# Stick-breaking attention in one core's three-block model: constant products split in halves, value projection moved among the heads

## What is computed

```
z = einsum(q_block, k_upto_end) * 64 ** -0.5
mask = s_pos < t_pos
log_1m = where(mask, log_sigmoid(-z), 0)
tail = cumsum(log_1m, reverse) - log_1m          # sum over s < j < t
w = where(mask, exp(log_sigmoid(z) + tail), 0)
y[t] = sum_s w[t, s] * v[s]
```

## Time and profile before

| | us |
|---|---|
| median of 3 runs (lowest to highest) | 3806.75 (3800.33 to 3807.62) |
| the profiled execution | 3799.45 |
| its span | 3798.1 |
| PE busy in the span | 3574.1 |
| DVE, ACT, POOL busy | 2016.2, 1440.3, 350.3 |
| the stage from the end of q and k to the first gate | 1664.5 to 1791.9 |

### The profile page before, as it was taken

How to read it: one execution, slowest core, us unless ns; L and a number is a source line. 1 busy time by engine, 2 the same in 40 slices (tenths; PEclk the granted TensorE clock), 3 DMA queues, 4 the chain that set the end, 5 groups by cost and what they waited for, 6 DMA issues and landing times. The chain is left out here.

```text
span 3798.1 us, 44034 instructions
## 1 busy us (share of the span) xinstructions
PE 3574.1 (94%) x16956; PEld 2892.0 (76%) x16956; DVE 2016.2 (53%) x3283; ACT 1440.3 (38%) x2555; POOL 350.3 (9%) x346
## 2 busy tenths in 40 slices
PE   8999989999998999989999989998899998989999
PEld 7877777877776887767887778877776777867877
DVE  4546465678436324731334466666465475563256
ACT  2224343355523223436223353354343232343244
POOL 1000000013001100012010100000000123111101
PEclk9999999999999999999999999999999999999999
DMA  6445311221223324420322232254201220132255
GB/s 235 181 172 178 118 45 52 72 67 34 95 89 107 132 94 135 164 66 12 106 80 72 95 100 95 95 173 142 86 23 49 72 78 12 39 112 88 93 180 166
DMA packets 106126, 380.15 MB, mean 100 GB/s; under 512 B 11760, under 2 KB 14592, under 8 KB 105792
## 3 DMA queue, kind: packets, MB, share of 16 engines
q1 hardware_dynamic: 100944, 364.86, 29.2%
q0 software_dynamic: 2896, 10.38, 0.9%
q10 hardware_dynamic: 2080, 2.10, 0.2%
HBM read 375.19 MB, written 2.10 MB: 99 GB/s over the span
## 5 line engine op out<-in xcount | busy, mean ns | idle before, releaser
L396 DVE TENSOR_TENSOR w_low<-ring,w_high 128x1024 fp32r<-128x1024 f32 x637 | 810.8, 1274 | 1011.0 <-ACT w_high L384 1003.4
L420 PE MATMUL bank<-x_low,w_high 128*128 128x512 f32 (+1 forms) x2560 | 999.9, 394 | 58.3 <-DVE w_low L396 15.9
L384 ACT ACTIVATE w_high<-ring 128x1024 fp32r<-128x1024 f32 x637 | 670.6, 1053 | 899.2 <-PE bank L420 377.6
L420 PE MATMUL bank<-x_high,w_low 128*128 128x512 f32 (+1 forms) x2560 | 988.4, 390 | 0.0
L420 PE MATMUL bank<-x_high,w_high 128*128 128x512 f32 (+1 forms) x2560 | 635.2, 386 | 0.0
L420 PEld LDWEIGHTS bank<-x_low,w_high 128*128 128x128 f32 x2560 | 494.7, 193 | 162.5 <-issue 23.9
L420 PEld LDWEIGHTS bank<-x_high,w_low 128*128 128x128 f32 x2560 | 495.6, 194 | 97.2 <-issue 1.4
L420 PEld LDWEIGHTS bank<-x_high,w_high 128*128 128x128 f32 x2560 | 466.4, 192 | 99.2 <-issue 1.9
L482 PE MATMUL bank<-w_low,x_high 128*128 128x512 f32 (+3 forms) x416 | 156.8, 377 | 1.3 <-ACT z_z L1693 1.3
L484 PE MATMUL bank<-w_high,x_high 128*128 128x512 f32 (+3 forms) x416 | 155.7, 374 | 0.0
L483 PE MATMUL bank<-w_high,x_low 128*128 128x512 f32 (+3 forms) x416 | 155.7, 374 | 0.0
(11 more groups left out here) (626 smaller groups left out, 5669.1 us busy)
## 6 DMA issues: line engine op xcount, KB each, us to landing
ring<-in_W SPq DMA_DIRECT2D x688, 512.0 KB, 3.5
f_hid<-in_xT ACTq DMA_DIRECT2D x2, 1024.0 KB, 11.6
X<-in_x POOLq DMA_DIRECT2D x1, 2048.0 KB, 10.7
out<-X SPq DMA_DIRECT2D x4, 512.0 KB, 4.2
const<-in_consts POOLq DMA_DIRECT2D x1, 1389.0 KB, 7.0
f_norm<-in_ln_g POOLq DMA_DIRECT2D x2, 512.0 KB, 8.6
f_norm<-in_ln_b POOLq DMA_DIRECT2D x2, 512.0 KB, 10.9
ring<-in_W SPq DMA_DIRECT2D x2, 432.0 KB, 3.1
```

The costliest lines, as they stand in the source:

```text
L384: ac.activation(b.UH[i % NU][:, 0:src.shape[1]], src, ACT.Copy).then_inc(*b.split.act.up("high", i))
L396: dv.tensor_tensor(b.UL[i % NU][:, 0:n], src, b.UH[i % NU][:, 0:n].bitcast(F32), SUB).then_inc(*b.split.dve.up("low", i))
L420: i = pe.matmul(out, w[:, k, c], v, start=n == 0 and q == 0, stop=last and q == 3 * K - 1)
```

## The change

1. The products of line 2085 are taken of two fp32r halves of `B1`: `BH` (high) and `BL` (low), against fp32r copies `nge`, `nones` of the constants, which are exact in that type. Identity and `neg` get fp32r copies as well. VectorE makes the halves of head r-1 in round r, `BH` over the place of `A1` and `BL` over that of `B1`; its semaphore `halves` takes the place of GpSimd's `sp` for TensorE. `A1` has three buffers where it had two.
2. The value projection `v2` moves from ahead of the rounds to round 1, after the scores of head 1. Its conversions (ScalarE, VectorE) and copies into `VP` move with it; TensorE waits for `v` only ahead of head 0's output, but waits for `k` ahead of the first scores.
3. In a round TensorE takes the scores first, then the log weights, then the output. ScalarE takes the absolute value, exponential and logarithm of head r first, then the exponential of the log weights of head r-2. VectorE splits outputs one round later, at the end of its round.

```diff
 def tensor_stick(b, s):
     pe.wait_ge(*s.gq.act.at("q", 3))
-    pe.wait_ge(*s.gq.dve.at("v", 3))
-    pe.wait_ge(*b.arrived("const2"))
+    pe.wait_ge(*s.gq.dve.at("k", 7))
     for r in range(8 + 3):
+        h = r            # scores, as before
...
+        if r == 1:
+            tensor_rows(b, s.gq, "v2", b.x, lambda t: b.bank(("v2", t), s.gq.dve.at("v", t)))
+            pe.wait_ge(*g.dve.at("signs"))
+        h = r - 2
...
+                pe.matmul(bank.ap[:, 0:wd], s.KP[:, j, l, c0:c0 + 128], s.QT[:, j, c0:512], start=True, stop=False)
+                pe.matmul(bank.ap[:, 0:128], s.eye, s.neg, start=False, stop=False)
+                if i == 0:
+                    pe.wait_ge(*g.dve.at("halves", h))
+                for jj in range(i, 4):
+                    sl = slice(OFF2[jj], OFF2[jj] + WID2[jj])
+                    sign, out = s.nge if jj == i else s.nones, bank.ap[:, 128 * (jj - i):wd]
+                    pe.matmul(out, sign, s.BL[h % 3][:, sl], start=False, stop=False)
+                    x = pe.matmul(out, sign, s.BH[h % 3][:, sl], start=False, stop=jj == 3)
...
+            if h == 0:
+                pe.wait_ge(*s.gq.dve.at("v", 3))
 def scalar_stick(b, s):
+            a1 = s.A1[h % 3]
+            if h >= 3:
+                ac.wait_ge(*g.pe.at("logw", h - 3, 3))
...
+        if r < 2:
+            for k in V2_AHEAD[r]:
+                scalar_ahead(b, ("v2", "w", k))
 def vector_stick(b, s):
+    for x, name in ((s.nge, "nge"), (s.nones, "nones"), (s.neg, "neg")):
+        dv.tensor_copy(x, b.const(name)).then_inc(*f.up())
+    dv.tensor_copy(s.eye, b.ident).then_inc(*f.up("signs"))
+    def halves(h):
+        b1, high, low = s.B1[h % 3], s.BH[h % 3], s.BL[h % 3]
+        dv.wait_ge(*g.pool.at("sp", h))
+        dv.tensor_copy(high, b1).then_inc(*f.up("high", h))
+        dv.wait_ge(*f.at("high", h))
+        dv.tensor_tensor(low, b1, high.bitcast(F32), SUB).then_inc(*f.up("halves", h))
...
+        if r < 2:
+            for k in V2_AHEAD[r][:1]:
+                vector_ahead(b, ("v2", "w", k))
+        if 1 <= r < 9:
+            halves(r - 1)
+        if r == 1:
+            for k in V2_AHEAD[r][1:]:
+                vector_ahead(b, ("v2", "w", k))
+            vector_v2(b, s)
```

More of the change, by code:

```diff
@@ L1911, in __init__ @@
         gates = Area(b, a.at)
-        self.A1 = [a.take("a2_a", 1280) for _ in range(2)]
-        self.B1 = [a.take("a2_b", 1280) for _ in range(3)]
+        over = Area(b, a.at)
+        self.A1, self.B1 = ([a.take(f"a2_{n}", 1280) for _ in range(3)] for n in "ab")
+        self.BH, self.BL = ([over.take(f"a2_b{n}", 1280, dtype=F32R) for _ in range(3)] for n in "hl")
         self.W1 = [a.take("a2_w", 1280) for _ in range(2)]
         self.sinc = a.take("a2_sinc", 128)
+        self.nge, self.nones, self.neg, self.eye = (a.take(f"a2_{n}", 128, dtype=F32R) for n in ("nge", "nones", "neg", "eye"))
         self.YAH, self.YAL = a.take("a2_yh", 4, 512, dtype=F32R), a.take("a2_yl", 4, 512, dtype=F32R)
@@ L2006, in tensor_qkv2 @@
         tensor_tile(b, g, ("q2", m), [("q2", m)], 0, b.x, bank.ap)
-    tensor_rows(b, g, "v2", b.x, lambda t: b.bank(("v2", t), g.dve.at("v", t)))
 def scalar_qkv2(b, s):
@@ L2016, in scalar_qkv2 @@
             ac.activation(s.QT[:, m, :], b.bk["q2", m], ACT.Copy, scale=0.125).then_inc(*g.act.up("q", m))
-    scalar_rows_ahead(b, "v2")
 def vector_qkv2(b, s):
@@ L2028, in vector_qkv2, with vector_v2 @@
             dv.tensor_copy(s.KP[64:128, m - 4, 1, :], b.bk["q2", m][64:128, :]).then_inc(*g.dve.up("k", m))
-    vector_rows_ahead(b, "v2")
+def vector_v2(b, s):
+    dv, g = b.nc.vector, s.gq
     dv.wait_ge(*g.pool.at("v_zero"))
@@ L2049 @@
 WID2 = [512, 384, 256, 128]
+V2_AHEAD = ((0,), (2, 4, 6))
 def tensor_stick(b, s):
@@ L2054, in tensor_stick @@
     pe.wait_ge(*s.gq.act.at("q", 3))
-    pe.wait_ge(*s.gq.dve.at("v", 3))
-    pe.wait_ge(*b.arrived("const2"))
+    pe.wait_ge(*s.gq.dve.at("k", 7))
     for r in range(8 + 3):
+        h = r
+        if h < 8:
+            j, l = h // 2, h % 2
+            for i in range(4):
+                bank = b.bank(("ss", h, i), g.dve.at("pos", h, i))
+                for e in bank.emptied:
+                    pe.wait_ge(*e)
+                c0 = 128 * i
+                pe.matmul(bank.ap[:, 0:WID2[i]], s.KP[:, j, l, c0:c0 + 128], s.QT[:, j, c0:512], start=True,
+                          stop=True).then_inc(*g.pe.up("scores", h, i))
+        if r == 1:
+            tensor_rows(b, s.gq, "v2", b.x, lambda t: b.bank(("v2", t), s.gq.dve.at("v", t)))
+            pe.wait_ge(*g.dve.at("signs"))
+        h = r - 2
+        if 0 <= h < 8:
+            j, l = h // 2, h % 2
+            for i in range(4):
+                bank = b.bank(("sw", h, i), g.act.at("w", h, i))
+                for e in bank.emptied:
+                    pe.wait_ge(*e)
+                c0, wd = 128 * i, WID2[i]
+                pe.matmul(bank.ap[:, 0:wd], s.KP[:, j, l, c0:c0 + 128], s.QT[:, j, c0:512], start=True, stop=False)
[7 more added lines that the diff above has]
+                    x = pe.matmul(out, sign, s.BH[h % 3][:, sl], start=False, stop=jj == 3)
+                x.then_inc(*g.pe.up("logw", h, i))
         h = r - 3
@@ L2071, in tensor_stick @@
                 b.drop(("so", j))
[L2072 to L2097, removed]
 def scalar_stick(b, s):
@@ L2102, in scalar_stick @@
     for r in range(8 + 2):
+        h = r
+        if h < 8:
+            a1 = s.A1[h % 3]
+            if h >= 3:
+                ac.wait_ge(*g.pe.at("logw", h - 3, 3))
+            for i in range(4):
+                ac.wait_ge(*g.pe.at("scores", h, i))
+                ac.activation(a1[:, OFF2[i]:OFF2[i] + WID2[i]], b.bk["ss", h, i][:, 0:WID2[i]],
+                              ACT.Abs).then_inc(*f.up("abs", h, i))
+            ac.wait_ge(*f.now())
+            ac.activation(a1, a1, ACT.Exp, scale=-1.0).then_inc(*f.up())
+            ac.wait_ge(*f.now())
+            ac.activation(a1, a1, ACT.Ln, bias=1.0).then_inc(*f.up("log", h))
+        if r < 2:
+            for k in V2_AHEAD[r]:
+                scalar_ahead(b, ("v2", "w", k))
         h = r - 2
@@ L2110, in scalar_stick @@
                               ACT.Exp).then_inc(*f.up("w", h, i))
[L2111 to L2123, removed]
 def vector_stick(b, s):
@@ L2129, in vector_stick @@
     dv.tensor_scalar(s.sinc, b.const("neg"), 0.0, None, ALU.is_equal).then_inc(*f.up("sinc"))
[L2130 to L2137, removed]
+    for x, name in ((s.nge, "nge"), (s.nones, "nones"), (s.neg, "neg")):
[7 more added lines that the diff above has]
+        dv.tensor_tensor(low, b1, high.bitcast(F32), SUB).then_inc(*f.up("halves", h))
+    for r in range(8 + 4):
         h = r
@@ L2146, in vector_stick @@
                                  MAX).then_inc(*f.up("pos", h, i))
+        if r < 2:
[7 more added lines that the diff above has]
+            vector_v2(b, s)
+        h = r - 4
+        if 0 <= h < 8 and h % 2:
+            j = h // 2
+            dv.wait_ge(*g.pe.at("out", h))
+            dv.tensor_copy(s.YAH[:, j, :], b.bk["so", j]).then_inc(*f.up("yhigh", j))
+            dv.wait_ge(*f.at("yhigh", j))
+            dv.tensor_tensor(s.YAL[:, j, :], b.bk["so", j], s.YAH[:, j, :].bitcast(F32), SUB).then_inc(*f.up("out", j))
 def gpsimd_stick(b, s):
@@ L2152, in gpsimd_stick @@
     for h in range(8):
-        a1, b1 = s.A1[h % 2], s.B1[h % 3]
+        a1, b1 = s.A1[h % 3], s.B1[h % 3]
         gp.wait_ge(*g.act.at("log", h))
```

## The result

| | before | after |
|---|---|---|
| median of the runs, us (lowest to highest) | 3806.89 (3800.33 to 3807.62), 4 runs | 3782.32 (3776.81 to 3790.68), 4 runs |
| profiled execution, us | 3799.45 | 3776.81 |
| from the end of the last q2 product to the first gate product, us | 127.1 | 104.7 |

The ratio is 0.9942, with a 95% interval from 0.9926 to 0.9958: faster, by 24.6 us between the medians where 24.7 was forecast. That the two agree to 0.1 us is luck: the same comparison made again, beside the last experiments, gives 18.2 us (3803.69 less 3785.45). The table's last line is the sharper one. It is read in the timeline of TensorE: from the last product of line 420 (start plus its step of 0.233 us) to the first product of the gates.

What follows compares the result with a forecast made beforehand. TensorE alone was taken to set the round of this stage, busy for all 11.70 us. The terms 12.5 + 3.5 + 10.4 - 1.7 = 24.7 us took the median 3806.75 to 3782.0, range 3773 to 3796.

Steps and rivals of the forecast that it cites:

- The constant products: TensorE's log weights: two fp32r matmuls per product cost 2.78 us a head against 4.34, saving 12.5 us over eight heads.
- The open price: Step of a 128 column fp32r product on TensorE, without a measured row: taken as 0.111 us, bounded above by 0.22.
- The first rival: Narrow fp32r matmuls on TensorE cost what float32 costs, 0.22 us: 14.2 us gained, 3792.6; chance 0.2.
- Identity times neg: Four 128 column products a head on TensorE fall from 0.22 to 0.111 us each, saving 3.5 us.
- The start: Value projection covers head 0's chain, so TensorE's 7.16 and 0.89 us waits and the lower clock's 2.3 go: 10.4 us.
- the one for k: New TensorE wait ahead of the first scores, for the copy of k's unit 7: 1.7 us lost.
- the cover for the conversions: v2's third and fourth units, converted by ScalarE and VectorE, are ready 5 and 3 us before TensorE needs them.
- the third rival: Conversions of v2 are late and the projection stands still in round 1; by 5 us: 3787; chance 0.05.
- The new order: Order of a round on TensorE and ScalarE, with banks of scores and exponentials: cost 0, bounds 0 to 2 us.
- The second rival: TensorE's wait moves to VectorE's halves, rounds stay near 11.7 us, only 8.7 us gained: 3798; chance 0.06.
- The slower rival: Short TensorE waits drop its clock to 1.2 GHz in the rounds; half of them would give 3821; chance 0.03.
- The sum: All terms for the stage together: 24.7 us gained, from the median 3806.75 to 3782.0.

Runs made afterwards that it cites:

- the last experiments: Changed kernel again (3785.45 us), beside changed kernel with output split first in VectorE's round and k awaited pair by pair (3783.97 us).
- the turned order: Changed kernel with a block's products taken all low halves first, then all high halves; 3791.57 us, stretch 104.7.
- the first experiment: Changed kernel with the constant products in plain float32 again, no halves of B1; 3795.9 us, ratio 0.9984 to before.
- the experiment: Changed kernel with VectorE's split of an output pair at the head of its round, not its end; 3788.85 us, stretch 102.1.
- the old order: Kernel before with fp32r halves alone, its order of a round kept and the value projection ahead of the rounds; 3799.37 us, ratio 0.9982.

## Why the prediction was right

**The constant products** were forecast at 12.5 us from steps of other widths. Taken back alone they cost 1.56 us a round, 12.5 in all. The open price, 128 columns in fp32r, came out at its lower bound, 0.11 to 0.12. The first rival (0.22, 3792.6 us) is refuted by that step and by the round of 9.73 us. The rule of the Trainium skill (TensorE: Matmul & The Clock Gate, Back-to-back issue gap) that gives 56 ns at 128 columns shows in single steps of 0.06 only; the turned order shows that the next matmul pays it back. The Trainium skill, TensorE: Matmul & The Clock Gate, section LDWEIGHTS (loading the stationary operand), gives a weight load as columns/1.2; by it 128 columns are an estimated 107 ns, and the steps of 0.11 us agree with that.

**Identity times neg** was forecast at 3.5 us, and 11.73 less the round of 11.29 us in the first experiment gives 3.5. With the products it took the log weights of a head from 7.40 to 5.36 us (1710.96 to 1716.32, where the output starts), 5.40 forecast.

**The start.** The waits of 7.16 and 0.89 us and the lower clock are gone, and the one for k came with 1.7 us (1662.8 to 1664.51). Right, and the cover for the conversions was there, though thinner than forecast: GpSimd's sums stretched VectorE's two passes from 1.23 to 3.2 us. The low half of the third unit was ready at 1676.63 and used at 1680.1, that of the fourth at 1684.0 and 1685.7: margins of 3.5 and 1.7 us where 5 and 3 were forecast. So the third rival (late conversions) did not come, by less than 2 us.

**The new order**, cost 0, bounds 0 to 2: here a term failed. The step went through the banks of scores and exponentials and took the held bank as merely absent. But when the pair's hold ends, the bank can come round for the third block of the log weights in the next round, as it does twice, and VectorE's read of it, moved one round later and behind the halves, was the last to free it: 2.1 us of waits, 2.5 of the stretch by the experiment. It lies a little beyond the bound given. It accounts for the 2.3 us that the stretch lacks. The same step's reason for the order was missing too: "At the end the order helps a wait that the trace doesn't have" is true of the kernel before, but with halves the old order waits in every round (118.0 us, against 114.0 with the new order, which has the 2.5 of the bank in it; the old order's first wait is 2.4 longer, and its rounds 0.64 each).

**The second rival** (the wait moves to the halves) did not happen in this order: the halves of head 1 are ready at 1696.95 and used at 1702.16, 5.2 us of cover, and no other head has less. In the old order it does happen, by 0.64 us a round. **The slower rival** fell: the granted clock is 1.00 through the rounds, two waits of 1.05 us included.

**The sum.** 12.5 + 3.5 + 10.4 - 1.7 = 24.7; less the 2.5 that the bank cost by its own experiment, 22.2, and the stretch's measured gain is 22.4. The median's 24.6 holds 2 us that the stretch does not have and that lie within the spread of the runs; without them the forecast would have been 2 us off.

## What to carry to other kernels

When a pass is put behind others on an engine, look up every buffer that the pass reads and ask who gets it next: a rotating pool of banks ties a late read to a product that has nothing to do with it. A longer chain (here halves behind GpSimd) wants to be laid against the other engine's work in the order of the round before it is called hidden, with what stands ahead of it in its own engine's program counted in: in the old order that was 2.3 us behind another head's maximum. And where an edit is worth 0.1%, read it in a stretch of the trace that repeats to 0.01 us, not in the whole time.

## What the runs showed of the hardware

VectorE's subtraction of two SBUF operands, started while GpSimd's sum runs, stands until the sum is done: the pass takes 3.20 us beside a sum and 1.23 us without. The Trainium skill says this in SBUF — State Buffer, section SBUF: two separate sides: an exclusive lock, whoever starts first keeps it for the whole instruction, for two SBUF inputs too when GpSimd reads SBUF; the trace agrees. I had not priced it, and by the margin of 1.7 us for the fourth unit I estimate that a start with 2 us less cover would have paid.

A matmul of 128 columns in fp32r, with weights of its own, costs 0.11 to 0.12 us on average in both orders that were tried; single steps of 0.06 us (128 columns) and 0.29 (512 columns, in place of 0.233) are two sides of one sum.
